# Loading the experts' down weights in pieces of 8 KB instead of 4 KB, one transfer a block, in a two-layer trunk with a mixture of experts

## What is computed

```python
def swiglu(h, w1, w3, w2):
    return (jax.nn.silu(h @ w1) * (h @ w3)) @ w2

def moe_swiglu(h, w_router, w1, w3, w2):
    logits = jnp.einsum('bsd,de->bse', h, w_router).astype(jnp.float32)
    top_val, top_idx = lax.top_k(logits, TOP_K)
    top_w = jax.nn.softmax(top_val, axis=-1)
    gates = jnp.sum(jax.nn.one_hot(top_idx, N_EXPERTS, dtype=jnp.float32) * top_w[..., None], axis=-2)
    out = jnp.zeros_like(h)
    for e in range(N_EXPERTS):
        out = out + gates[..., e:e + 1].astype(h.dtype) * swiglu(h, w1[e], w3[e], w2[e])
    return out
```

## Time and profile before

| | us |
|---|---|
| median of 3 runs | 1305.41 (1304.89 to 1305.57) |
| span of the profiled execution, first to last instruction | 1300.1 |
| median of the runs less that span | 5.3 |
| PE busy, share of the span | 1254.0, 96% |
| DVE busy | 366.3, 28% |
| ACT busy | 246.1, 19% |
| bytes moved | 430.77 MB in 132102 packets, mean 331 GB/s |

### The profile page before, as it was taken

The page is one execution under the profiler, slowest core; times in us unless marked ns, Lnnn a source line. Parts: engine busy times, 40 slices in busy tenths (PEclk is TensorE's granted clock), DMA queues, the critical chain, the costliest instruction groups (busy, mean ns, idle before and its releaser), DMA issues.

```text
span 1300.1 us, 29767 instructions
## 1 busy us (share of the span) xinstructions
PE 1254.0 (96%) x13303; PEld 732.6 (56%) x13303; DVE 366.3 (28%) x484; ACT 246.1 (19%) x328; POOL 23.0 (2%) x38
## 2 busy tenths in 40 slices
PE   9999999999999999999999999999799999999775
PEld 6998888888989823543433644443243453354222
DVE  4777644444667520110010111011012001001002
ACT  5654544333573300000000000000000000000001
POOL 3000000000100000000000000000000000000000
PEclk9999999999999999999999999999999999999998
DMA  9842744423856899999999999999999999999995
GB/s 312 297 155 104 266 177 176 176 89 115 285 181 235 346 409 404 407 360 408 408 408 408 408 407 408 408 408 408 409 408 408 408 402 409 399 409 408 402 409 210
DMA packets 132102, 430.77 MB, mean 331 GB/s; under 512 B 12407, under 2 KB 18839, under 8 KB 131842
## 3 DMA queue, kind: packets, MB, share of 16 engines
q1 hardware_dynamic: 130354, 423.49, 83.9%
q0 software_dynamic: 1616, 5.33, 1.1%
HBM read 427.72 MB, written 2.11 MB: 331 GB/s over the span
## 4 chain that ended last, share of the span: by engine, by line
PE 86%; DMA 11%; SPq 1%; DVE 1%; ACT 1%; issue 0%; POOL 0%; POOLq 0%; DVEq 0%
PE psum L1901 34%; PE psum L1921 16%; PE psum L1422 9%; PE psum L1424 9%; PE psum L1423 9%; DMA ring<-in_moe_w 8%; DMA ring<-in_moe_w_end 2%; PE psum L1638 1%; PE psum L1875 1%; PE psum L1958 1%; PE psum L1850 1%; PE psum L1441 1%; SPq L494 0%; PE psum L1774 0%; PE psum L1597 0%; SPq L504 0%
## 5 line engine op out<-in xcount | busy, mean ns | idle before, releaser
L1901 PE MATMUL psum<-ring,xe 128*32 128x512 f32 (+1 forms) x5376 | 519.3, 541 | 19.9 <-DMA ring<-in_moe_w 14.9
L1901 PEld LDWEIGHTS psum<-ring,xe 128*32 128x32 f32 x5376 | 168.5, 110 | 350.7 <-issue 270.8
L1921 PE MATMUL psum<-ring,gT 128*32 128x256 f32 x4640 | 260.6, 381 | 11.1 <-DMA ring<-in_moe_w 11.0
L1921 PEld LDWEIGHTS psum<-ring,gT 128*32 128x32 f32 x4640 | 147.9, 110 | 127.5 <-issue 20.4
L1281 DVE TENSOR_TENSOR gate<-gate,psum 128x768 f32<-128x768 f32 (+3 forms) x32 | 24.6, 767 | 527.2 <-ACT gate L825 527.2
L920 DVE TENSOR_TENSOR wlo<-raw,whi 128x2048 fp32r<-128x2048 f32 (+1 forms) x66 | 145.3, 2229 | 58.7 <-ACT whi L651 58.4
L825 ACT ACTIVATE gate<-psum 128x768 f32<-128x768 f32 (+3 forms) x32 | 21.1, 661 | 614.2 <-PE psum L1901 614.2
L651 ACT CAST whi<-raw 128x2048 fp32r<-128x2048 f32 (+1 forms) x66 | 120.2, 1862 | 56.9 <-PE psum L1424 32.5
L1422 PE MATMUL psum<-whi,f_hi 128*128 128x512 f32 (+1 forms) x320 | 123.8, 387 | 1.1 <-DVE wlo L920 0.9
L1424 PE MATMUL psum<-whi,f_lo 128*128 128x512 f32 (+1 forms) x320 | 121.4, 379 | 0.0
L1423 PE MATMUL psum<-wlo,f_hi 128*128 128x512 f32 (+1 forms) x320 | 121.3, 379 | 0.0
(11 more groups left out here) (249 smaller groups left out, 795.7 us busy)
## 6 DMA issues: line engine op xcount, KB each, us to landing
ring<-in_moe_w SPq DMA_DIRECT2D x608, 512.0 KB, 14.4
raw<-in_ffn_w SPq DMA_DIRECT2D x33, 1024.0 KB, 5.6
ring<-in_moe_w_end SPq DMA_DIRECT2D x64, 512.0 KB, 14.7
raw<-in_w_mix_in SPq DMA_DIRECT2D x21, 1024.0 KB, 7.5
raw<-in_w_mix_out SPq DMA_DIRECT2D x8, 1024.0 KB, 5.3
raw<-in_w_mix_in SPq DMA_DIRECT2D x4, 544.0 KB, 6.0
x<-in_x SPq DMA_DIRECT2D x2, 512.0 KB, 4.3
raw<-in_w_mix_in SPq DMA_DIRECT2D x2, 512.0 KB, 6.4
```

What stands on the lines that cost most here:

```text
L1901: ins = mm(banks(j, n)[o:o + 32, g, 0:2 * q].rearrange("p (i b c) -> p i b c", i=2, c=64), rows_[:, k * CAP + 32 * g:k * CAP + 32 * (g + 1 ...
L1921: ins = mm(bank[bk][32 * q:32 * (q + 1), at_:at_ + 256], gT[j % 2][:, a:a + 32], w[:, o:o + 256], start=j == 0 and n == 0 and at_ == 0, st ...
```

## The change

A down block now comes from a group of 512 rows of w2, of which partition p holds rows 4p to 4p + 3. Two blocks share a group: the first holds rows 4p and 4p + 1, the second 4p + 2 and 4p + 3. These two rows lie behind each other in memory, so one transfer of 128 pieces of 8 KB loads the block; the pieces of neighbouring partitions start 16 KB apart. The semaphore gets 16 instead of 32 for a down block, and the count that PE waits for is summed over the slot's uses. The up products read the up blocks in runs of 128 columns instead of 64 and the transposes read at a step of 4 elements instead of 2, so that the features meet the new rows. Products, blocks, slots, their order and the bytes are the same.

```diff
-        def fills(f):
-
-            return f // RING + 1
+        def is_down(f):
+
+            e, p = divmod(f % PER_SWEEP - 8, PER_EXPERT)
+            end = (36, 37) if e < EXPERTS - 1 else (32, 33)
+            return e >= 0 and (p in range(8, 12) or p in range(20, 24) or p in range(28, 32) or p in end)
+
+        def landings(f):
+
+            return sum(16 if is_down(g) else 32 for g in range(f % RING, f + 1, RING))
...
-                w = moe_w2[0].rearrange("e (n p k) d -> n p e k d", p=P, k=2)
+                w = moe_w2[0].rearrange("e (n p k) d -> n p e k d", p=P, k=4)
                 for b in range(QUARTER[j] // 64):
                     to, until = free_slot(f + b, turn)
-                    for k in range(2):
-                        src = w[4 * j + b, :, ds(who, 1), k, :].rearrange("p e d -> p (e d)")
-                        sp.dma_start(to[:, D * k:D * (k + 1)], src
-                                     ).wait_op(moe_used, until, "sem-ge").then_inc(moe_full[ring_slot(f + b)], 16)
+                    h2 = 2 * (b % 2)
+                    src = w[2 * j + b // 2, :, ds(who, 1), h2:h2 + 2, :].rearrange("p e k d -> p (e k d)")
+                    sp.dma_start(to[:, :], src
+                                 ).wait_op(moe_used, until, "sem-ge").then_inc(moe_full[ring_slot(f + b)], 16)
...
-                    ins = nc.vector.transpose(gT[j % 2][:, a:a + n].rearrange("p (b k s) -> p b k s", k=2, s=32),
-                                              gate[j % 2][:, o:o + n].rearrange("p (b c k) -> p b k c", c=32, k=2))
+                    ins = nc.vector.transpose(gT[j % 2][:, a:a + n].rearrange("p (b k s) -> p b k s", k=4, s=32),
+                                              gate[j % 2][:, o:o + n].rearrange("p (b c k) -> p b k c", c=32, k=4))
...
-                pe.wait_ge(moe_full[ring_slot(f)], 32 * fills(f))
+                pe.wait_ge(moe_full[ring_slot(f)], landings(f))
...
-                                ins = mm(banks(j, n)[o:o + 32, g, 0:2 * q].rearrange("p (i b c) -> p i b c", i=2, c=64),
+                                ins = mm(banks(j, n)[o:o + 32, g, 0:2 * q].rearrange("p (i b c) -> p i b c", i=2, c=128),
                                          rows_[:, k * CAP + 32 * g:k * CAP + 32 * (g + 1)],
-                                         w[:, kk, :, :].rearrange("p i (b t c) -> p i b t c", t=4, c=64)[:, :, :, t, :],
+                                         w[:, kk, :, :].rearrange("p i (b t c) -> p i b t c", t=4, c=128)[:, :, :, t, :],
```

## The result

The changed kernel takes 1297.52 us (median of 5 runs, 1294.93 to 1300.11) where the kernel before takes 1305.41 (5 runs): 0.9942 of it, with a 95% interval of 0.993 to 0.9955. That is 7.6 us by the ratio; 6.9 were forecast. Set beside other kernels on a chip a second time it gave 0.9942 again (0.9928 to 0.9957).

The account below looks back on a forecast made before the run. From about 570 us the always-full DMA load queue was taken to set the end. 98 down blocks at 70 ns gave -6.9 us, all other terms 0: 1305.41 to 1298.5 us, range 1292.5 to 1305.0.

Parts of the forecast that it names:

- the early down blocks: Fourteen down blocks before the last 98, where slots or PE hold the pace; faster loads there counted at nothing.
- The price of the pieces: Down-weight loads on SP's queue: eight fewer pieces per engine and block save 70 ns, 6.9 us over 98 blocks.
- the slope: Piece price from 2 KB loads at 387 GB/s against 4 KB ones: 8.8 ns fixed part, 70 ns a block.
- the direct row: Piece price from the one transfer with 8 KB pieces, on POOL's queue: 11 ns, 90 ns a block.
- PE's reads: Up products on PE reading runs of 128 elements instead of 64; claimed to cost 0.
- The transposes: DVE's transposes at a step of 4, 979 ns before; 0 since hidden, 0.5 us if twice as long and uncovered.
- The smaller fixed part: Rival for the down loads: 43 ns a block, 4.2 us saved, 1301.2 us; chance 0.13.
- the cut pieces: Rival: SP's queue cuts 8 KB pieces at 4 KB, so 0.9 us saved, 1304.5; chance 0.13 shared with byte pacing.
- the byte-paced queue: Rival: bytes alone pace the load queue, so 0.9 us saved, 1304.5; chance 0.13 shared with the cut at 4 KB.
- the collision: Rival: down-block reads 16 KB apart hit the same parts of memory, 13.7 us slower, 1319.1; chance 0.10.
- a gain beyond the slope: Rival: down loads save beyond 12 us if end marks cost more than seen; chance 0.04.
- PE's cover: PE's idle time for following faster loads: 12.5 us in 880:980 and 19.6 us behind 1190; claimed sufficient.

Follow-up runs that it names:

- the half-loaded kernel: Only the first row of each pair of down weights loaded and read twice, against one transfer of 8 KB pieces with the old dealing; 1259.21 us, 0.9653 of the kernel before.

## Why the prediction was right

*What bounds.* The reading of the queue held: from about 570 us it never stood still, a saving in it moved the end by about the same amount, and adding to it (2 KB pieces) moved the end the other way by the price of the pieces.

That the early down blocks bring nothing was not tried alone, but the packets in the traces bear on it. They give the time at which SP's queue has moved a given number of bytes. Where the kernel before stands at 580 us, the changed kernel is 0.9 us ahead of it. The two kernels with the new dealing and 4 KB pieces, which save nothing, are 0.5 and 0.6 us ahead there, so this is hardly more than scatter. The kernel with 2 KB pieces is 2.0 us behind at 560 us and only 0.4 at 580: what it had lost was made good where slots hold the pace. At 1280 us the changed kernel is 6.9 us ahead and the one with 2 KB pieces 14.2 behind. Nearly all of both differences arises behind 580 us, where 94 of the 98 blocks are issued: 6.0 and 13.8 us, or 7.9 and 9.2 ns a piece.

*The price of the pieces.* The term was 70 ns a block. The ratios give 77 (60 to 93 by the interval) and 71, the rate of the earlier trace rows against the one after gives 75. These don't decide between the slope's 70 and the direct row's 90. That the slope came so near was in part luck: its 387 GB/s came from one stretch of 6 us, and with its neighbours, 395 and 372, the same sum gives a fixed part of 5.3 or 15.6 ns. The kernel with 2 KB pieces says which was fair: with a third of its bytes in such pieces it moves 401 GB/s, 2.615 us a block, so a down block took 3 x 2.615 - 2 x 2.570 = 2.705 us, which is 388 GB/s. The lower bound by the best stretch of 2 KB, 43 ns, and "only bytes count" are excluded by the kernel with 2 KB pieces.

*PE's reads, SP's issues, the arrival waits* at nothing: right. Up blocks cost 20.60 us for eight at every length of run, and one transfer instead of two changed nothing by itself.

*The transposes* at nothing: right for the time, though they became dearer by 68%. They stayed hidden, as the new dealing alone shows with 0.9996, and PE waits for no transpose in the changed kernel either. The text had allowed for twice the price without expecting it.

*The rivals.* The smaller fixed part, the cut pieces, the byte-paced queue and the collision each have a run or a row against them; so has a gain beyond the slope through the end marks, which with the transfers are worth 1.4 us at most. The Trainium skill's figure of about 3 cycles a packet (DMA: Bandwidth & Descriptors, "Why small descriptors are slow (HBM only)") comes, at the 850 MHz of its fabric, to an estimate of 3.5 ns. This kernel pays 8.0 to 9.7 ns a piece, so the measurement decides.

*The base.* The prediction read 5.3 us as what lies around the span. Every run that lists both has its time only 1.7 to 2.0 us above its span. So the profile with a span of 1300.1 us came from an execution of about 1302 us, not from one of 1305.41. The sum starts from the median, so the forecast of the time isn't touched. The forecast span, 1293.2 us, should have been some 3.5 us longer, and that the profile of the changed kernel has 1293.6 is luck: its execution took 1295.39 us, and the median run, 1297.52 us, had a span of 1295.6.

*Where it was off.* Two of its signs came out differently. PE's waits were to fall to about 25 us and stand at 28.4, and the rate in 980:1190 was to be 412 and is 409. The second is the base: that stretch had 406 before, not 408, and 3 GB/s more is nearly the share that was meant. The first is, at least in part, the error that the half-loaded kernel shows: the idle time in the views is smaller than the time that PE loses to its weights, so it also shrinks by less than the end moves (3.6 against 6.5 us). In the fifth expert, from its first product to the next expert's, PE now needs 973.58 - 878.63 = 95.0 us instead of 99.7, 4.7 less, while its counted waits there fall by 3.6, from 12.4 to 8.8. It would have mattered for a change large enough to use up PE's cover, where the sum would have stopped 10 us or more too early.

## What to carry to other kernels

When the DMA engines are full and their queue never stands still, count pieces as well as bytes: here each piece costs some 8 to 10 ns beside its bytes, between 2 and 8 KB alike, and merging pieces that are neighbours in memory pays, while merging two transfers without it brought nothing that could be told. Look first whether the present layout already has neighbours to merge; this change needed no new dealing for its gain. And take the price of a size that isn't in the trace from the slope between two that are, over as long a stretch as there is, not from the idle time that the change is to remove.

## What the runs showed of the hardware that was not expected

- **A step of 16 bytes.** The transposes of DVE on 768 columns of float32 take 978 ns reading at a step of 1, 979 at 2 and 1645 to 1649 at a step of 4. The Trainium skill (SBUF — State Buffer, "Door 1: The DMA port swizzle") speaks of lines of 16 bytes, of which two hits are needed for full rate. By that rule a step of 2 is free and a step of 4 is not, and the trace agrees. The same passage says that float32 can be read at a step of 4 for free; here that step costs 68%, so the measurement decides. That the lines are the cause is not shown: only these three steps were run.
- **The idle time of PE is less than what it loses** where it waits for every block: 12.5 us of idle PE stood in 880:980 us, and 17.0 us were lost there; a block behind a wait stands at 1.97 us instead of 1.72.
- **Transfers and end marks are free as far as can be told** while the queue is full: half as many of both for the down blocks left the time at 1.000 of what it was (0.9989 to 1.001), 1.4 us less at most.
